# Neighbourhood attention by pairs of heads, laid between the projections of heads 8 to 15 and the out projection

## The reference, cut to what matters

```
def neighbourhood_attention(h, w_qkv, q_norm, k_norm, rpb, w_out):
    # 256 tokens are a grid of 4 rows x 64 columns; 16 heads of 64
    qkv = (h @ w_qkv).reshape(bsz, rows, GRID_W, 3, NA_HEADS, NA_HEAD_DIM)
    q = rmsnorm(qkv[:, :, :, 0], q_norm) * (NA_HEAD_DIM ** -0.5)
    k = rmsnorm(qkv[:, :, :, 1], k_norm)
    v = qkv[:, :, :, 2]
    ...
    s = einsum('bxqhd,brxkhd->bhxqrk', q_blk, k_blk)
    s = s + where(col_valid, rpb[row_rel][col_rel], -inf)
    pr = softmax(s over the window)
    o = einsum('bhxqrk,brxkhd->bxqhd', pr, v_blk)
    return out @ w_out
```

## Time and profile before

| | |
|---|---|
| median of 3 runs | 1695.6 us |
| profiled execution, its own time | 1696.47 us |
| its span | 1694.7 us |
| busy in the span: PE, PEld, DVE, ACT, POOL | 99%, 85%, 64%, 53%, 4% |
| granted clock of TensorE | 0.997 on average |

### The profile page before, as it was taken

One profiled execution on the slowest core, in us unless ns is written; L12 is line 12 of the kernel. 1 busy time (PEld: TensorE's weight loads), 2 busy tenths in 40 slices (PEclk: granted clock), 3 DMA queues, 4 the chain that ended last, 5 costly groups with the idle time before them and its releaser, 6 DMA issues.

```text
span 1694.7 us, 22995 instructions
## 1 busy us (share of the span) xinstructions
PE 1681.2 (99%) x9366; PEld 1436.8 (85%) x9366; DVE 1076.8 (64%) x1332; ACT 898.8 (53%) x1279; POOL 74.1 (4%) x79
## 2 busy tenths in 40 slices
PE   8999999999999999999999999999999999999998
PEld 6888899998788888888888678888889999988886
DVE  5554678999965545755456866555655578776643
ACT  5443567777864435644355655444553456655432
POOL 0000000000100000000002500000000000000000
PEclk9999999999999999999999999999999999999999
DMA  9655567666466555776555226555565533556551
GB/s 296 190 182 186 159 182 217 184 181 217 153 197 195 196 167 181 193 238 208 177 170 199 88 75 209 178 197 165 189 194 163 161 107 120 173 192 184 183 185 64
DMA packets 243977, 300.58 MB, mean 177 GB/s; under 512 B 9248, under 2 KB 175520, under 8 KB 243872
## 3 DMA queue, kind: packets, MB, share of 16 engines
q1 hardware_dynamic: 238224, 289.25, 54.1%
q10 hardware_dynamic: 5648, 9.85, 2.0%
HBM read 297.96 MB, written 1.11 MB: 176 GB/s over the span
## 4 chain that ended last, share of the span: by engine, by line
PE 97%; DVE 1%; issue 1%; ACT 1%; DMA 0%; ACTq 0%; DVEq 0%
PE bank L562 93%; PE bank L565 4%; DMA h<-in_x 0%; DVE st L2191 0%; DVE sr L1838 0%; ACT whi L1326 0%; DVE wlo L1838 0%; DVE sr L2198 0%; DVE hTlo L1841 0%; DVE xn L1841 0%; DVE h L1841 0%; ACT kT L1326 0%; ACT nv L1326 0%; ACT hThi L1326 0%; DVE xn L1890 0%
## 5 line engine op out<-in xcount | busy, mean ns | idle before, releaser
L1838 DVE TENSOR_TENSOR wlo<-raw,whi 128x2048 fp32r<-128x2048 f32 (+2 forms) x284 | 620.6, 2190 | 333.6 <-ACT whi L1326 333.6
L1326 ACT ACTIVATE whi<-raw 128x2048 fp32r<-128x2048 f32 (+2 forms) x284 | 518.2, 1832 | 250.4 <-PE bank L562 246.9
L562 PE MATMUL bank<-whi,hThi 128*128 128x512 f32 x1072 | 426.0, 397 | 0.0
L562 PE MATMUL bank<-wlo,hThi 128*128 128x512 f32 x1072 | 418.8, 391 | 0.4 <-DVE wlo L1838 0.4
L562 PE MATMUL bank<-whi,hTlo 128*128 128x512 f32 x1072 | 403.6, 391 | 0.0
L562 PE MATMUL bank<-hThi,whi 128*128 128x256 f32 x888 | 253.4, 285 | 0.0
L562 PE MATMUL bank<-hThi,wlo 128*128 128x256 f32 x888 | 251.2, 283 | 0.0
L562 PE MATMUL bank<-hTlo,whi 128*128 128x256 f32 x888 | 251.2, 283 | 0.0
L562 PEld LDWEIGHTS bank<-whi,hThi 128*128 128x128 f32 x1072 | 201.9, 188 | 43.1 <-issue 3.2
L562 PEld LDWEIGHTS bank<-whi,hTlo 128*128 128x128 f32 x1072 | 201.8, 188 | 43.2 <-DVE hTlo L1841 0.3
L562 PEld LDWEIGHTS bank<-wlo,hThi 128*128 128x128 f32 x1072 | 202.1, 188 | 41.3 <-DVE wlo L1838 1.5
(11 more groups left out here) (214 smaller groups left out, 1881.6 us busy)
## 6 DMA issues: line engine op xcount, KB each, us to landing
raw<-in_ffn_w_gu SPq DMA_DIRECT2D x172, 512.0 KB, 4.9
raw<-in_ffn_w_down SPq DMA_DIRECT2D x40, 1024.0 KB, 5.0
raw<-in_w_in SPq DMA_DIRECT2D x30, 1024.0 KB, 5.3
raw<-in_ssd_w_in SPq DMA_DIRECT2D x16, 1024.0 KB, 5.6
raw<-in_ssd_w_in SPq DMA_DIRECT2D x32, 512.0 KB, 5.5
raw<-in_w_up SPq DMA_DIRECT2D x16, 1024.0 KB, 5.4
raw<-in_w_down SPq DMA_DIRECT2D x16, 1024.0 KB, 5.0
raw<-in_na_w_qkv SPq DMA_DIRECT2D x12, 1024.0 KB, 5.2
```

What stands on the lines that cost most here:

```text
L562: return T.e.matmul(out, lhsT, rhs, start=start, stop=stop, skip_group_check=skip)
L1326: return e.activation(out, in_, ACT.Identity, **kw)
L1838: return e.tensor_tensor(out, a, b, op)
```

## The change: what it does

- The column blocks are projected in the order 0, 2, 4, 1, 3, 5 (`NA_CHUNKS`), so q, k and v of heads 0 to 7 are there first. The plan of the DMA loads follows, and takes the tiles of w_out in the order (0,0), (1,0), (0,1), (1,1).
- Attention goes by pairs p = 0 to 7 (heads 2p and 2p+1). `scores` and `values` issue the matmuls of the two heads in turn. The groups of a pair stand between half tiles (12 matmuls, one half of the tokens) of the projections of blocks 1, 3 and 5 for pairs 0 to 3, and between pieces of the out projection for pairs 4 to 7.
- On VectorE the addition of the bias and the maximum become one instruction, `tensor_tensor_reduce`, for each half of the queries; it writes minus the sum, and the exponentials take scale -1. The compiled list shows it as two `ISA` rows, the second 128x1.
- GpSimd makes the bias ahead for eight heads instead of three (`bias_of`), between its roots.
- The root's users are moved: VectorE makes the mean squares of a block (`means`), splits a tile, and only then scales (`unit`).
- The outputs of pairs 0 to 3 go to new buffers `noThi` and `noTlo`, since `hThi` and `hTlo` are still read by the projections.
- Each engine's order is written out line by line instead of following `na_steps`.

The diff, cut to its core:

```diff
@@ plan_of @@
-    for c in range(6):
+    for c in NA_CHUNKS:
         for k in range(2):
             p.add(("qkv", c, k), ...)
-    for c, k in QUARTERS:
+    for c, k in NA_OUT:
+NA_CHUNKS = (0, 2, 4, 1, 3, 5)
+NA_OUT = ((0, 0), (1, 0), (0, 1), (1, 1))
@@ tensor: natt @@
+            def scores(p):
+                for j in range(2):
+                    clear(nabank["scores", p, j])
+                ...
                 for t in range(2):
-                    done = mm(bank_half(b, t), qT[p0:p0 + 64, blk, t * P:(t + 1) * P], kT[p0:p0 + 64, blk, :], True, True)
+                    for j in range(2):
+                        z = slice(64 * j, 64 * j + 64)
+                        done = mm(bank_half(nabank["scores", p, j], t), qT[z, p, t * P:(t + 1) * P], kT[z, p, :], True, True)
+                        if t:
+                            done.then_inc(*sig("nscore", 2 * p + j))
+            def values(p):
+                ...
                 for kt in range(2):
+                    for j in range(2):
+                        hd = 2 * p + j
+                        done = mm(banks[b][64 * j:64 * j + 64, 0:256], v[:, kt, hd * 64:hd * 64 + 64], pt[:, j, kt * 256:kt * 256 + 256],
+                                  kt == 0, kt == 1, True)
...
+            transposes(1, 0, (6, 7))
+            half_tile("qkv", 4, 1, 1)
+            scores(0)
+            half_tile("qkv", 1, 0, 0)
+            half_tile("qkv", 1, 0, 1)
+            scores(1)
+            half_tile("qkv", 1, 1, 0)
+            turn_p(0)
+            half_tile("qkv", 1, 1, 1)
+            values(0)
+            scores(2)
+            half_tile("qkv", 3, 0, 0)
+            turn_p(1)
+            half_tile("qkv", 3, 0, 1)
+            values(1)
+            scores(3)
+            half_tile("qkv", 3, 1, 0)
+            turn_p(2)
+            turned(0)
+            half_tile("qkv", 3, 1, 1)
+            values(2)
...
+            half_tile("qkv", 5, 1, 1)
+            scores(4)
+            half_tile("nout", 0, 0, 0)
+            scores(5)
+            half_tile("nout", 0, 0, 1)
+            turn_p(4)
+            scores(6)
+            half_tile("nout", 1, 0, 0)
+            values(4)
+            turn_p(5)
+            half_tile("nout", 1, 0, 1)
+            values(5)
+            scores(7)
+            out_part(0, (0,))
+            turn_p(6)
+            out_part(0, (1,))
+            values(6)
+            out_part(1, (0,))
+            turn_p(7)
+            out_part(0, (2,))
+            values(7)
+            out_part(1, (1,))
+            out_part(0, (3,))
...
@@ vector: natt @@
+            def logits(p):
+                for j, hd in enumerate(heads_of(p)):
...
-                    tt(s, banks[nabank["scores", hd]], bm[:, i, :, :].rearrange("p t c -> p (t c)"), ALU.add).then_inc(*sig("nbias", hd))
-                    V.wait_ge(*at("nbias", hd))
-                    e.tensor_reduce(nm[:, 2 * i:2 * i + 2], split3(s), AX, ALU.max, negate=True).then_inc(*sig("nmax", hd))
+                    for t in range(2):
+                        done = e.tensor_tensor_reduce(s[:, t * 256:t * 256 + 256], bank_half(nabank["scores", p, j], t), bias_of(hd)[:, t, :],
+                                                      -1.0, TOP, ALU.add, ALU.min, nm[:, t:t + 1])
+                    done.then_inc(*sig("nmax", hd))
...
+            logits(2)
+            split(0)
+            means(3)
+            take("qkv", 3, 0)
+            normalise(2)
+            unit(3)
+            logits(3)
+            split(1)
+            take("qkv", 3, 1)
+            normalise(3)
...
+            take("qkv", 5, 1)
+            logits(4)
+            take("nout", 0, 0)
+            logits(5)
+            normalise(4)
+            normalise(5)
+            logits(6)
...
@@ gpsimd: natt @@
+            roots(0)
+            G.wait_ge(*at("d_tb", 1))
+            G.wait_ge(*at("d_c2"))
+            bias(0)
+            bias(1)
+            roots(1)
+            bias(2)
+            bias(3)
+            bias(4)
+            bias(5)
+            roots(3)
+            bias(6)
+            bias(7)
+            roots(4)
```

More of the change, by code:

```diff
@@ L16 @@
 BIG = 1e30
+TOP = 3e38
 NRAW, NSPL = 4, 3
@@ L248, in give @@
         self.held.discard(b)
[L251 to L264, removed]
-def na_banks():
[L268 to L280, removed]
+def na_banks():
+    uses = [("scores", 0), ("scores", 1), ("turn", 0), ("values", 0), ("scores", 2), ("turn", 1), ("values", 1), ("scores", 3), ("turn", 2),
+            ("turned", 0), ("values", 2), ("turn", 3), ("values", 3), ("turned", 1), ("scores", 4), ("scores", 5), ("turn", 4), ("scores", 6),
+            ("values", 4), ("turn", 5), ("values", 5), ("scores", 7), ("turn", 6), ("values", 6), ("turn", 7), ("values", 7)]
+    out, i = {}, 0
+    for what, x in uses:
+        for j in range(1 if what == "values" else 2):
+            out[what, x, j] = 4 + i % 4
+            i += 1
     return out
@@ new lines, in out_part, with turned @@
+            def out_part(c, ks, ts=(0, 1)):
+                label = ("nout", c, 1)
+                if 0 in ks:
+                    held[label] = take(*label)
+                for k in ks:
+                    for t in ts:
+                        last = products(label, k, t, False, k == 3)
+                        if k == 3:
+                            last.then_inc(*sig(*half(label, t)))
+            def turned(which):
+                transposes(which, 1, [nabank["turned", which, j] for j in range(2)])
@@ new lines, in gained @@
+            def gained(which):
+                with_gains(which, 1, [nabank["turned", which, j] for j in range(2)])
+            take("qkv", 0, 0)
+            take("qkv", 0, 1)
+            squares(0)
+            take("qkv", 2, 0)
+            take("qkv", 2, 1)
+            squares(1)
+            with_gains(0, 0, (4, 5))
+            take("qkv", 4, 0)
+            take("qkv", 4, 1)
+            with_gains(1, 0, (6, 7))
+            values(0, pair(2))
+            take("qkv", 1, 0)
+            exps(0)
@@ new lines, in natt @@
+            take("qkv", 1, 1)
+            exps(1)
+            evict(0)
+            split(0)
+            squares(3)
+            take("qkv", 3, 0)
+            exps(2)
+            evict(1)
+            split(1)
+            take("qkv", 3, 1)
+            exps(3)
+            evict(2)
+            gained(0)
+            split(2)
+            squares(4)
+            take("qkv", 5, 0)
+            evict(3)
+            split(3)
+            take("qkv", 5, 1)
+            gained(1)
+            values(1, pair(5))
```

355 lines of the change are left out of this document (207 added, 148 removed).

## The result

The changed kernel takes 1678.5 us (median of four runs, 1677.87 to 1678.64) against 1695.9 us (four runs, 1694.48 to 1696.22): a ratio of 0.9898, with a 95% interval of 0.9886 to 0.991. That is 17.4 us less. The profiled execution took 1677.87 us, 18.6 less than the one before.

What follows compares the result with a forecast made beforehand. TensorE was taken as the bound, busy 1681.2 of 1694.7 us. Its list 17.8 us shorter, less waits of 1.9 and 0.9, gave 15.0 us gain and 1680.6 us; range 1677 to 1688.

Steps and rivals of the forecast that it cites:

- the signs: Expected timeline evidence: pairs as x8 in about 1.14 and 1.1 us, feed-forward 15 us earlier, waits only at named places.
- no waits: Rival: T near 0.42 and GpSimd's roots fall well, so gain 17 to 17.8 us, 1677.8 to 1678.6; chance 0.20.
- The list of TensorE: TensorE's instructions in the attention stage: 43.7 us before, 25.9 after, so 17.8 us shorter.
- The price of the places: Attention groups at 18 places between projections: 13 at 0.2 us and five at 0.1, 3.1 us together.
- T: VectorE's fused instruction with its accumulator read, start to start: taken as 0.55 us, between 0.42 and 0.87.
- Place 1: TensorE's transposes of pair 2, waiting for VectorE's `oTlo` of pair 1: about 1.9 us.
- Place 2: TensorE's transposes of pair 4, waiting for VectorE's logits and normalising: 0.9 us.
- nothing above 0.5 us: Claim, used against the slower rival, that no VectorE pass over 256 columns in the trace exceeds 0.5 us.
- VectorE holds it back: Rival: T at 0.87, waits of 4.5 and 3.5 us and 0.4 elsewhere, gain 9.4, 1686.2 us; chance 0.15.
- The rival that pairs do not lie side by side: Rival: scores and values on TensorE cost 8 x 2.05 us more, gain 1.4, 1694.2 us; chance 0.04.
- The slower rival: VectorE bounds the stage, its fused instruction running as several passes; no gain from T = 1.5 us; chance 0.03.

Runs made afterwards that it cites:

- the run with the heads apart: Changed kernel with each pair's heads one after the other and one full 128x128 dummy transpose between them, in scores and values; 1698.8 us, ratio 1.0022.
- The unfused run: Changed kernel with the logits of a head again as one addition and one reduction on VectorE; 1682.1 us, ratio 0.9923.
- the old rotation with pairs: Kernel before, its rotation of heads behind the projections kept, with scores and values issued by pairs and the fused VectorE instruction; 1690.7 us, ratio 0.9971.
- pairs alone: Kernel before, rotation kept, with only TensorE's scores and values issued by pairs; 1695.1 us, ratio 1.0001.
- head after head: Changed kernel with a pair's scores and values issued as all of head 0, then all of head 1, nothing between; 1678.2 us, ratio 0.9902.
- the run with the double reduction: Changed kernel with addition and reduction again separate, and each head's reduction done twice; 1688.9 us, ratio 0.9959.
- the run with the scaling at once: Changed kernel with the scaling directly behind its means again for three of the four q and k blocks; 1679.2 us, ratio 0.9906.

## Why the prediction was right, and where it was off

The time, 1678.5 us, lies in the range (1677 to 1688), and so do the signs, but the case that came true is the first rival, "no waits" (1677.8 to 1678.6), with its chance of 0.20, not the forecast of 1680.6. Two errors lie against each other in the number: the list was counted 0.8 us too short, the waits 2.8 us too long.

The list of TensorE: forecast 17.8 us shorter, measured 17.0. Both hold the 1.84 us that TensorE waited in the stretch of before: the prediction took all 41.0 us as list, so the instructions alone got 15.2 us shorter, and 1.8 are waits that went. Adding up, between each pair of ordinary matmuls with attention or transposes of q and k between them, what exceeds their usual 0.227 us gives 46.67 us before and 27.58 after, 19.1 less. The other 2.1 us are lost by the projections' own matmuls: the first one behind each such group takes 0.1 us over its usual time, 0.6 us in all behind 6 groups before and 2.2 behind 22 after, and a few hundredths each on those that follow make the rest. The price of the places, taken at 3.1, was thus about 0.8 too low, and the run with the heads apart confirms the large term by itself.

T: bounds 0.42 to 0.87, taken 0.55, measured 0.35. This is the step of the working that failed, and it lay outside its bounds. The lower bound added ScalarE's 0.09 for reading an accumulator; on VectorE the read runs beside the next instruction and is free. Without it the bound would have been 0.33.

Place 1: forecast a wait of 1.9 us, measured none, with 1.5 of slack, so VectorE was 3.4 us earlier than counted. T explains 1.6 of it (eight of 0.20), and the two waits for the port and the root, 1.8 together (less 0.3 of overlap), did not occur: in the timeline above the scalings of the fourth block, q of heads 8 to 15, start at 935.89 without waiting. The collision was there, but GpSimd bore it: its two roots took 4.41 us beside the tile in place of 2 x 1.64, the tile took the 2.29 that it takes alone, and the tile and the normalising that the new order puts between gave the roots their time. The run that moves the scaling back brings 1.3 us of wait to this place, so the roots were a real danger there. Place 2: forecast 0.9, measured none; eight of 0.20 account for it. The unfused run, with T at 0.68, had 1.5 us there. What I had not seen is that a wait there can also cost clock, about as much again. Nor had I seen that GpSimd's bias slows VectorE's scalings and not only its tiles: "nothing above 0.5 us" over 256 columns was a wrong reading of the trace of before, where this scaling of 128x256 takes 736 ns at most (350 in the median). In the changed kernel that cost little; in the old rotation with pairs it is what held the run back.

The rival "VectorE holds it back" got its 0.15 for a real mechanism: at T = 0.68 it costs 4.5 us, at 1.03 11.4. The rival that pairs do not lie side by side (1694.2) is refuted by the timeline, and its price was tested: with the heads apart the stage is 16.6 us longer without the dummies, where 16.4 was counted. The slower rival would, by its own sum, have needed T of 1.5.

A whole place of values or scores costs 0.2 us, as taken: three fewer shorten the stage by 0.6. The Trainium skill's rule that a change of the tiling mode drains TensorE ("TensorEngine Tiling (Array Packing)", Tiling Modes, Key Properties) has no size; a cost of 0.2 us a place agrees with it, though no run shows the drain by itself, and it was no obstacle.

## What to carry to other kernels

Two heads' matmuls of this size that use different halves of the array's rows (scores) or columns (values) cost one if nothing of the full array stands between them; whether they alternate was of no account with four records for each half, but pairing pays only where the engine that feeds them keeps up. When the bound is shortened, recount the next engine with its collisions: here pairs alone gave nothing, pairs with a shorter VectorE step 4.7 us (12.5 of stage with GpSimd's bias out of the way), and the spread among other TensorE work all 17. A wait on an otherwise full TensorE can cost twice its length when the clock falls with it, as after one of 1.5 us here; after one of 1.3 us it did not fall.

## What was not expected of the hardware

The read of VectorE's accumulator (82 ns) runs wholly beside the next instruction: the fused instruction and its read together take 0.34 to 0.35 us from start to start. With head after head, the first instruction for the other half of the array starts 0.01 us behind the first of the four records that were issued ahead of it for this half. VectorE's scaling of 128x256, 351 ns on average with GpSimd still, averages 678 ns where GpSimd's bias always starts with it. A halt of TensorE of 1.5 us (to 970.66) goes with a mean granted clock of 0.70 from 970 to 975, one of 3.9 us (to 976.63) with 0.51 and 0.81 in the two stretches of 5 us from 975 on; but one of 1.9 us in the run with the double reduction (to 945.2) and one of 1.3 us in the run with the scaling at once (to 943.2) left it at 1.00. What decides between these is open.
